# Two-layer hybrid decoder trunk: the MLP's up products as Strassen block products

## The chip, the cores and the metric
The kernel runs on one core of one Trainium2 chip. The metric is the device time of one execution in microseconds (us); lower is better. TensorE is called PE here, VectorE DVE, ScalarE ACT, GpSimd POOL, SyncE SP.

## The reference, cut to what matters
1024 prompt tokens and 32 sample tokens (T = 1056 in all) of 1024 features pass an even layer (GLA and S5 mixer) and an odd layer (conv and RG-LRU mixer). Behind each mixer stands the part that is changed here:

```python
def channel_mixer(x, g_norm, w_up, w_down):
    h = jnp.square(jax.nn.relu(rmsnorm(x, g_norm) @ w_up))
    return h @ w_down        # w_up (1024, 4096), w_down (4096, 1024), float32
```

## The kernel before, in words
Features lie on the 128 partitions: the residual `X` is 8 rows (KT) of 1056 token columns, cut into 3 chunks of CH = 352. A float32 product is made of three passes in a rounded type: with x = XH + XL and w = WH + WL, it adds WH*XH, WH*XL and WL*XH. ACT makes the rounded part (`hi`), DVE the rest (`lo_w`, a subtraction). Inside `product` each matmul has a 128x128 weight block and 352 columns.

Weights come as 128x1024 tiles from one stream in HBM into `WR`, two raw slots. SP waits until a slot's tile has been split (semaphore `w_ready`) and loads the next. The split parts lie in `WH` and `WL`, four slots. Each layer's MLP is 4096 hidden units, 32 tiles of 128 (FT), taken in 16 groups (HG) of two. PE makes the two up tiles (8 weight blocks each, all three chunks), and then the 8 down products of the group before: each adds two hidden tiles into one of 8 output rows. Products go by turns into the two PSUM halves of `acc` (3 banks each). Eight banks exist; `ms` has the other two.

DVE evicts an up product with ReLU and the norm's factor `RS` (`evict`), ACT squares it into `HH`, DVE makes the rest `HL`, and the down products are added to `X` by DVE (`add_to_residual`). Each engine runs its own written order, and semaphores that count up connect them; the groups are hardware loops (`Fori`). The norm's factor per token is computed from squares summed across the rows (`norm_sum`) and is applied after the product, so that the up products can start before it is known.

Ahead of each MLP, `residual(r)` runs on ACT and DVE beside the output projection (`oute`, `outo`, one product for each output row): DVE adds a row, ACT squares it and makes `XH`, DVE makes `XL` and sums the squares. `lam()` makes a small constant of the odd layer and stands before the first MLP.

Of the kernel before, what the change touches and what calls it, by code (L numbers as in the profile page):

```python
# [19 lines left out]
P = 128  # L20
# [67 lines left out]
MLP_TILES = 2 * FT  # L88
ODD_W = ["xb0", "xb1", "xb2"]
for _n in range(1, KT):  # L90
# [5 lines left out]
               + [f"mlp0_{n}" for n in range(MLP_TILES)]  # L96
               + ODD_W
               + [f"outo{m}" for m in range(KT)] + [f"mlp1_{n}" for n in range(MLP_TILES)])
# [8 lines left out]
for _n in range(KT):  # L107
    if _n < KT - 1:
# [5 lines left out]
            + [f"mlp0_{n}" for n in range(HG * (2 + KT))] + _odd + [f"outo{m}" for m in range(KT)]  # L114
            + [f"mlp1_{n}" for n in range(HG * (2 + KT) - KT)])
S5R = index(["ab0t", "ab0r", "cd0a", "cd0b", "ab1t", "ab1r", "cd1a", "cd1b", "ef0a", "ef0b", "ab2t", "ab2r",
             "cd2a", "cd2b", "ef1a", "ef1b", "ab3t", "ab3r", "cd3a", "cd3b", "ef2a", "ef2b", "ef3a", "ef3b"])
M0 = STREAM["mlp0_0"]
# [5 lines left out]
for _name, _n in (("norm0", KT), ("z", 4), ("zg", 4), ("o", 4), ("norm1", KT), ("norm2", KT),  # L124
                   ("mix", 8), ("norm3", KT)):
    SPLIT[_name] = _at
    _at += _n
# [20 lines left out]
def trunk_kernel(nc, x_t, w_stream, par_d, par5_d, cst_d, w_a2, w_ri, st_gla, odd_lru, odd_conv,  # L148
# [8 lines left out]
    with ExitStack() as ctx:  # L157
# [22 lines left out]
        WL = sb(ctx, "WL", [P, SLOTS, 1024], F32R)  # L180
        TT = sb(ctx, "TT", [P, 4, T])
        par = sb(ctx, "par", [P, NPAR])
        cst = sb(ctx, "cst", [P, NCST])
# [56 lines left out]
        XP = sb(ctx, "XP", [P, 3 + SEQ + 7 * NB])  # L240
        WRI = sb(ctx, "WRI", [P, 2, 2, P])
# [3 lines left out]
        CN = sb(ctx, "CN", [P, KT, 3 * (1 + NB)])  # L245
        acc = ctx.enter_context(nc.psum_tensor("acc", [P, 2, NCH, 512], F32))
# [57 lines left out]
        h_sq, h_ready = sem("h_sq"), sem("h_ready")  # L304
# [71 lines left out]

        ident, tri = c_("ident"), c_("tri").rearrange("p (i n) -> p i n", i=NBL)
# [21 lines left out]
        def _(sp):  # L399
# [5 lines left out]
            sp.dma_start(cst[:, :], cst_d).then_inc(cst_in, 16)  # L405
# [118 lines left out]
            at = POOL_LOADS  # L524
            while (NT - at) % 4:
                load_w(at, at % RAW)
                at += 1
            with sp.Fori(0, (NT - at) // 4) as i:
                for j in range(4):
                    n = at + j  # L530
                    split_wait(sp, n - RAW, i * 4)
                    sp.dma_start(WR[:, n % RAW, :], w_stream[i * 4 + n]).then_inc(w_in[n % RAW], 16)
# [9 lines left out]
        @block.gpsimd  # L542
        def _(pool):
            for n in range(POOL_LOADS):
                if n == STREAM["eo1"]:
                    done_wait(pool, "glu3")
                    pool.memset(QM[1][:, :], 0.0).then_inc(qm_zero, 1)
                if n >= RAW:
                    split_wait(pool, n - RAW)
                pool.dma_start(WR[:, n % RAW, :], w_stream[n]).then_inc(w_first[n % RAW], 16)  # L550

            for m in range(1, KT):
# [8 lines left out]
        def _(pe):  # L561
# [394 lines left out]

            def mlp(layer, r):
                w0, t0 = STREAM[f"mlp{layer}_0"], ACC[f"mlp{layer}_0"]
                h0 = FT * layer
                flat = lambda x: 0  # L960
                HOPS = [(lambda k, b=b: HH[:, b + k, :], lambda k, b=b: HL[:, b + k, :]) for b in (0, 2)]

                def up(n, t, per, xn=None, ks=None):

                    split_wait(pe, n, per(4))
                    if t >= 2:
                        pe.wait_ge(acc_read[t % 2], per(5) + t // 2)
                    product(t, lambda k: n % SLOTS, lambda k: k * P, XOPS, xn=xn, ks=ks)

                def down(hready, half, base_w, base_t, per):  # L970

                    split_wait(pe, base_w + 1, per(4))
                    pe.wait_ge(h_ready, hready)
                    for m in range(KT):
                        t = base_t + m
                        pe.wait_ge(acc_read[t % 2], per(5) + t // 2)
                        product(t, lambda k: (base_w + k) % SLOTS, lambda k: m * P, HOPS[half], nk=2)

# [14 lines left out]
                def last_down(hready, base_w, base_t):  # L993

                    split_wait(pe, base_w + 1)
                    pe.wait_ge(h_ready, hready)
                    for c in range(NCH):
                        for m in range(KT):
                            q = c * KT + m
                            b = q % 6  # L1000
                            if q in (0, 3):
                                t = base_t - 2 + (base_t + b // 3) % 2
                                pe.wait_ge(acc_read[t % 2], t // 2 + 1)
                            if q >= 6:
                                pe.wait_ge(fin_read, q - 5)
                            for k in range(2):
                                for i, (w, x) in enumerate(PASSES):
                                    last = mm(acc[:, b // 3, b % 3, 0:CH], w[:, (base_w + k) % SLOTS, m * P:(m + 1) * P],
                                              HOPS[1][x](k)[:, cols_of(c)], k == 0 and i == 0, k == 1 and i == 2)
# [8 lines left out]
                up(w0, t0, flat, SPLIT[f"norm{r}"], ORDER if r == 1 else None)  # L1018
                norm_sum(r)
                up(w0 + 1, t0 + 1, flat)  # L1020
                with pe.Fori(0, HG // 2 - 1) as i:
                    per = lambda x: i * (2 * x)
                    for j in range(2):
                        for e in range(2):
                            up(w0 + 2 + 4 * j + e, t0 + 2 + 10 * j + e, per)
                        down(i * 4 + (h0 + 2 * j + 2), j, w0 + 4 + 4 * j, t0 + 4 + 10 * j, per)
                a = HG - 2
                for e in range(2):
                    up(w0 + 2 + 4 * a + e, t0 + 2 + 10 * a + e, flat)
                down(h0 + 2 * a + 2, 0, w0 + 4 + 4 * a, t0 + 4 + 10 * a, flat)  # L1030
                if layer == 0:
                    down(h0 + 2 * a + 4, 1, w0 + 6 + 4 * a, t0 + 12 + 10 * a, flat)
                else:
                    last_down(h0 + 2 * a + 4, w0 + 6 + 4 * a, t0 + 12 + 10 * a)
# [14 lines left out]

            project("xb0", "xb0", xn=SPLIT["norm2"])  # L1050
            norm_sum(2)
# [19 lines left out]
        def last_down(layer, k):  # L1071

            return f"mlp{layer}_{2 * HG + KT * (HG - 1) + k}"

        X_FROM = [None, None, lambda k: last_down(0, k), lambda k: f"outo{k}"]
# [8 lines left out]
        def _(act):  # L1084
# [39 lines left out]

            def residual(r):

                def square(i, k):
                    if i >= 4:
                        act.wait_ge(ssq_add, SSQ_N * (r - 1) + i - 3)
                    act.activation(TT[:, (i - 1) % 3 if i else 3, :], X[:, k, :], ACT.Square).then_inc(sq_done, 1)  # L1130
# [4 lines left out]
                if r == 1:  # L1135
                    for j in range(KT):
                        if j == KT - 1:
                            for e in range(4, KT - 1):
                                act.wait_ge(x_free, e - 3)
                                x_hi(e, ORDER[e])  # L1140
                        read_wait(act, f"oute{j}")
                        if j < 4 or j == KT - 1:
                            x_hi(j, ORDER[j])
                        square(j, ORDER[j])
                        if j % 2:
                            hi(M0 + j // 2)
                else:
                    for m in range(KT):
                        if r == 3 and m == KT - 1:
                            for k in range(KT - 1):  # L1150
                                act.wait_ge(x_free, 3 + KT - 1 + k + 1)
                                x_hi(k, k)
                        read_wait(act, X_FROM[r](m))
                        if r == 2 and m == 0:
                            act.wait_ge(h_ready, FT)
                        if r == 2 or m == KT - 1:
                            x_hi(m, m)
                        square(m, m)
                        if r == 3:
                            hi(STREAM[f"outo{m}"] + SLOTS)  # L1160
                if r == 2:
                    hi(M0 + MLP_TILES + 2)
                    hi(M0 + MLP_TILES + 3)
# [7 lines left out]
            def last_norm():  # L1171
# [8 lines left out]
                act.wait_ge(h_ready, 2 * FT)  # L1180
# [301 lines left out]
            def mlp(layer):  # L1482
                w0, t0, h0 = STREAM[f"mlp{layer}_0"], ACC[f"mlp{layer}_0"], FT * layer

                def hidden(t, per5, hcount, slot, u, first=False):

                    act.wait_ge(acc_read[t % 2], per5 + (t // 2 + 1))
                    act.activation(HH[:, slot, :], TT[:, u, :], ACT.Square).then_inc(h_sq, 1)  # L1488
                    if not first:
                        act.wait_ge(h_ready, hcount - 1)  # L1490
# [1038 lines left out]
```

## Time and profile before

| | |
|---|---|
| runs | 2280.03, 2280.75, 2290.98 us (median 2280.75) |
| profiled execution, its span | 2288.8 us (the page gives no other time for it) |
| PE busy | 2258.5 us, 13982 matmuls |
| DVE busy | 1198.0 us |
| ACT busy | 648.3 us |
| POOL busy | 23.1 us, 39 instructions |
| HBM traffic | 120.62 MB read, 18.99 MB written |

The span is the time from the first to the last recorded instruction of one execution. Busy times of different engines lie beside each other and are not to be added. A matmul's recorded duration (some 320 ns) is longer than the distance to the next one, since they are pipelined: the rate is read from a chain piece's length divided by its count.

### The profile page before, as it was taken

The page shows a single profiled execution, that of the slowest core. Times are in us where ns is not written, and L with a number is a line of the kernel's source. Part 1 is how long each engine was busy: PE and PEld are TensorE (multiplying, and loading weights), DVE is VectorE, ACT ScalarE, POOL GpSimd, SP SyncE. Part 2 cuts the span into 40 slices and gives each one's busy share as a digit, 9 for nine tenths or more (in the row PEclk, how much of TensorE's full clock was granted, in tenths as well). Part 3 has the DMA queues.
Part 4 walks back from the last instruction along what each step waited for, and adds up shares of the span by engine and source line. Part 5 has one row for each costly group of instructions (what it writes and reads, how often), then busy time and mean ns, then how long its engine had stood idle before and what let it go on. Part 6 is the DMA issues. An engine that isn't in the chain of part 4 may idle for free.

```text
span 2288.8 us, 32453 instructions
## 1 busy us (share of the span) xinstructions
PE 2258.5 (99%) x13982; PEld 2195.0 (96%) x13982; DVE 1198.0 (52%) x1338; ACT 648.3 (28%) x706; POOL 23.1 (1%) x39
## 2 busy tenths in 40 slices
PE   8999999999999999999999999999999999999997
PEld 8998788999999999999999998999999999999996
DVE  8777675644443444344458766544444434443445
ACT  5323632541111111111125556242111111111113
POOL 0000000000000000000000000000000000000001
PEclk9999999999999999999999999999999999999999
DMA  4334224511111111111111111111111111111102
GB/s 173 110 98 135 86 73 132 183 46 46 46 47 45 46 46 40 51 46 46 37 56 40 42 51 40 52 38 50 43 46 46 40 51 46 46 37 55 46 28 76
DMA packets 59129, 140.69 MB, mean 61 GB/s; under 512 B 6416, under 2 KB 30640, under 8 KB 59056
## 3 DMA queue, kind: packets, MB, share of 16 engines
q1 hardware_dynamic: 52720, 121.84, 16.4%
q0 software_dynamic: 3888, 14.16, 1.8%
q10 hardware_dynamic: 2448, 3.64, 0.5%
q8 instruction: 56, 0.92, 0.2%
q14 instruction: 17, 0.14, 0.0%
HBM read 120.62 MB, written 18.99 MB: 61 GB/s over the span
## 4 chain that ended last, share of the span: by engine, by line
PE 93%; DVE 4%; ACT 1%; issue 1%; DMA 0%; DVEq 0%; POOL 0%; ACTq 0%; POOLq 0%
PE acc L563 88%; PE ms L563 2%; DVE TT L1617 1%; PE acc L812 1%; DVE XL L1620 0%; DMA WR<-in_w_stream 0%; PE acc L890 0%; PE ms L660 0%; PE acc L827 0%; PE ms L617 0%; PE acc L823 0%; PE acc L835 0%; DVE XL L1617 0%; DVE HB L2362 0%; DVE X L1620 0%
## 5 line engine op out<-in xcount | busy, mean ns | idle before, releaser
L563 PE MATMUL acc<-XH,WH 128*128 128x352 f32 x2608 | 853.4, 327 | 9.2 <-ACT XP L1239 2.5
L563 PE MATMUL acc<-XL,WH 128*128 128x352 f32 x2608 | 840.0, 322 | 0.0
L563 PE MATMUL acc<-XH,WL 128*128 128x352 f32 x2584 | 833.9, 323 | 0.0
L1617 DVE TENSOR_TENSOR X<-X,acc 128x1056 f32<-128x1056 f32 (+1 forms) x288 | 343.2, 1193 | 370.6 <-PE acc L563 370.6
L563 PEld LDWEIGHTS acc<-XH,WH 128*128 128x128 f32 x2608 | 492.0, 189 | 21.9 <-issue 15.9
L563 PE MATMUL acc<-HH,WH 128*128 128x352 f32 x1536 | 496.6, 323 | 1.4 <-DVE X L1617 1.4
L563 PE MATMUL acc<-HH,WL 128*128 128x352 f32 x1536 | 495.9, 323 | 0.0
L563 PE MATMUL acc<-HL,WH 128*128 128x352 f32 x1536 | 495.3, 322 | 0.0
L563 PEld LDWEIGHTS acc<-XL,WH 128*128 128x128 f32 x2608 | 494.6, 190 | 0.2
L563 PEld LDWEIGHTS acc<-XH,WL 128*128 128x128 f32 x2584 | 487.3, 189 | 0.0
L1114 ACT ACTIVATE WH<-WR 128x1024 fp32r<-128x1024 f32 x177 | 182.8, 1049 | 624.0 <-PE acc L563 561.6
L1620 DVE SCALAR_TENSOR_TENSOR TT<-acc,RS 128x1056 f32<-128x1056 f32 x64 | 80.5, 1257 | 418.8 <-PE acc L563 410.3
L563 PEld LDWEIGHTS acc<-HH,WH 128*128 128x128 f32 x1536 | 288.4, 188 | 3.1 <-issue 1.7
L563 PEld LDWEIGHTS acc<-HL,WH 128*128 128x128 f32 x1536 | 288.3, 188 | 1.3
L563 PEld LDWEIGHTS acc<-HH,WL 128*128 128x128 f32 x1536 | 288.6, 188 | 0.0
L1488 ACT ACTIVATE HH<-TT 128x1056 fp32r<-128x1056 f32 x64 | 69.6, 1087 | 584.5 <-DVE TT L1620 584.5
L1617 DVE TENSOR_TENSOR WL<-WR,WH 128x1024 fp32r<-128x1024 f32 (+1 forms) x179 | 214.8, 1214 | 23.3 <-ACT WH L1114 22.7
L1617 DVE TENSOR_TENSOR HL<-TT,HH 128x1056 fp32r<-128x1056 f32 x64 | 80.3, 1255 | 72.4 <-ACT TT L1491 72.4
L1491 ACT ACTIVATE TT<-TT 128x1056 f32<-128x1056 f32 x64 | 68.4, 1069 | 0.0
L1130 ACT ACTIVATE TT<-X 128x1056 f32<-128x1056 f32 x24 | 25.9, 1078 | 66.5 <-DVE X L1617 66.5
L1620 DVE SCALAR_TENSOR_TENSOR XL<-X,par,XH 128x1056 fp32r<-128x1056 f32 x32 | 41.0, 1312 | 5.8 <-ACT XH L1087 3.2
L1617 DVE TENSOR_TENSOR TT<-TT 128x1056 f32<-128x1056 f32 x29 | 36.4, 1256 | 12.6 <-ACT TT L1130 12.2
(337 smaller groups left out, 1337.1 us busy)
## 6 DMA issues: line engine op xcount, KB each, us to landing
WR<-in_w_stream SPq DMA_DIRECT2D x152, 512.0 KB, 3.3
WR<-in_w_stream POOLq DMA_DIRECT2D x27, 512.0 KB, 4.1
X<-in_x_t SPq DMA_DIRECT2D x8, 528.0 KB, 9.6
LA<-in_x_t SPq DMA_DIRECT2D x24, 176.0 KB, 2.5
xz_scratch<-LA SPq DMA_DIRECT2D x24, 176.0 KB, 1.8
X<-xz_scratch SPq DMA_DIRECT2D x8, 528.0 KB, 5.6
out_y_t<-X SPq DMA_DIRECT2D x12, 352.0 KB, 2.4
u_scratch<-UR SPq DMA_DIRECT2D x4, 576.0 KB, 3.0
```

The lines of the kernel that those rows point to most:

```text
L563: return pe.matmul(out, lhs, rhs, start=start, stop=stop)
L812: last = pe.matmul(glb[0:keys, GLB[b], i * 2 * BL:(i + 1) * 2 * BL], KX[:, b, i * GC:i * GC + keys], QM[p][:, at:at + 2 * BL], start=True, ...
L1114: act.activation(WH[:, n % SLOTS, :], WR[:, n % RAW, :], ACT.Copy).then_inc(w_hi, 1)
L1130: act.activation(TT[:, (i - 1) % 3 if i else 3, :], X[:, k, :], ACT.Square).then_inc(sq_done, 1)
L1488: act.activation(HH[:, slot, :], TT[:, u, :], ACT.Square).then_inc(h_sq, 1)
L1491: act.activation(TT[:, 2 + u, :], TT[:, u, :], ACT.Square).then_inc(h_sq, 1)
L1617: return dve.tensor_tensor(out, a, b, op)
L1620: return dve.scalar_tensor_tensor(out=out, in0=a, scalar=scalar, in1=b, op0=op0, op1=op1)
```

## The change: Strassen's seven products in place of eight for two token chunks
For the up products the 8 weight blocks (K) of a hidden tile pair are cut into halves of 4, the two hidden tiles are the rows, and token chunks 0 and 1 the columns of a 2 by 2 block product. In Winograd's form it takes 7 products of 4 blocks each. Chunk 2 is computed as before (`p1` and `p2`, for tile 0 into bank `B_F0`, for tile 1 into `B_F1`). Four of its eight weight units are sums or differences of blocks; POOL makes them, four per group. Three of the products add up in one PSUM bank `B_CHAIN` in a row, and ACT copies the bank (`snapshot`) between them; the products in `B_P24` and `B_P3` are added to these copies by DVE (`c11`, `c12`, `p5`, `c22`, `c21`), which then applies ReLU.

The token operands (36 parts of 352 columns, some of them differences of chunks and rows) are made once per layer in `residual_mlp`, which takes the place of `residual` before an MLP. Parts lie in the rows of `XH` and `XL` and in spare places.

Weights are now split in units of 512 columns into a ring of 6 half tiles in three of the four slots of `WH`/`WL`. A group has 12 units: 8 up (u0 to u7), 4 down (d0 to d3). The two raw slots have names F0 and F1, and the MLP has a stream of its own (`w_mlp`). The squares of the hidden tiles and their rounding have become two ACT steps, and only one pair of hidden tiles is kept. `lam()` and the loads of the odd layer's states stand after the first MLP.

The diff, cut to its core and set in the order of the engines:

```diff
+        def up_source(j):
+            return (W_A11, W_SUM, W_A12, W_SUM, W_SUM, W_A11, W_A21, W_A22)[j]
+        def down_source(j):
+            return WR[:, :, 2 * P * j:2 * P * (j + 1)]
+F0, F1 = 1, 0
+AFTER = {"u0": 2, "u1": 3, "u2": 5, "u3": 6, "u4": 7, "u5": 8, "u6": 9, "u7": 11,
+         "d0": 13, "d1": 15, "d2": 17, "d3": 19}
+        W_A11, W_A12 = WR[:, F0, 0:UNIT], WR[:, F0, UNIT:2 * UNIT]
+        W_A21, W_A22 = WR[:, F1, 0:UNIT], WR[:, F1, UNIT:2 * UNIT]
@@ SP @@
+                def load(slot, n, units):
+                    sp.wait_ge(u_ready[layer], units)
+                    sp.dma_start(WR[:, slot, :], w_mlp[layer, n]).then_inc(raw_in[layer][slot], 16)
+                with sp.Fori(0, HG - 2) as i:
+                    load(F0, i * 4 + 4, i * STEP_UNITS + (8 + 6))
+                    load(F1, i * 4 + 5, i * STEP_UNITS + (8 + 8))
+                    load(F0, i * 4 + 6, i * STEP_UNITS + (8 + 12))
+                    load(F1, i * 4 + 7, i * STEP_UNITS + (8 + 12))
...
@@ POOL @@
+                def sums(units, earlier, raws, count):
+                    pool.wait_ge(raw_in[layer][F1], raws)
+                    if earlier is not None:
+                        pool.wait_ge(u_ready[layer], earlier)
+                    pool.tensor_tensor(W_SUM, W_A21, W_A22, ALU.add).then_inc(u_sum, 1)
+                    pool.wait_ge(u_ready[layer], units + 2)
+                    pool.tensor_tensor(W_SUM, W_SUM, W_A11, ALU.subtract).then_inc(u_sum, 1)
+                    pool.wait_ge(u_ready[layer], units + 4)
+                    pool.tensor_tensor(W_SUM, W_A12, W_SUM, ALU.subtract).then_inc(u_sum, 1)
+                    pool.wait_ge(u_sum, count)
+                    pool.tensor_tensor(W_A11, W_A11, W_A21, ALU.subtract).then_inc(u_sum, 1)
...
@@ PE, one group: 11 segments of 4 blocks x 3 passes (waits left out) @@
+                    segment(B_CHAIN, u0, "b11", True, False, True, wait=first)
+                    segment(B_F0, u0, "p1", True, False, wait=first)
+                    segment(B_CHAIN, u0 + 1, "t1", False, False, True, wait=first)
+                    segment(B_P24, u0 + 2, "b21", True, True, wait=first)
+                    segment(B_F0, u0 + 2, "p2", False, True, wait=first)
+                    segment(B_CHAIN, u0 + 3, "t2", False, False, True, wait=first)
+                    segment(B_P3, u0 + 4, "b22", True, True, wait=first)
+                    segment(B_CHAIN, u0 + 5, "t3", False, True, True, wait=first)
+                    segment(B_F1, u0 + 6, "p1", True, False)
+                    segment(B_P24, u0 + 7, "n4", True, True, wait=first)
+                    segment(B_F1, u0 + 7, "p2", False, True)
...
+                    down(16, units + 8, lambda m: evs + (3 if m == 0 else 6 if m == 1 else 5 + m), i * 2 + 2)
@@ PE, first group, before its first p1 @@
+                        read_wait(pe, "oute7" if layer == 0 else "outo7")
...
@@ ACT, one group (hi: round a unit; m + n waits for segment n, from 12 on for down products) @@
+                    for u in range(2):
+                        rounded(u, i * 2 + (u + 1), m)
+                    snapshot(layer, 0, m + 1, e)
+                    up_hi(layer, 5, 13, m, None, i * 4 + 4)
+                    up_hi(layer, 6, 14, m + AFTER["u0"], i * 32 + 32, None)
+                    snapshot(layer, 1, m + 3)
+                    up_hi(layer, 7, 15, m + AFTER["u1"], i * 32 + 32, None)
+                    snapshot(layer, 2, m + 6)
+                    down_hi(layer, 0, 16, m + AFTER["u2"], i * 32 + 48)
+                    down_hi(layer, 1, 17, m + AFTER["u3"], i * 32 + 48)
+                    down_hi(layer, 2, 18, m + AFTER["u4"], i * 32 + 48)
+                    squared(0, i * 2 + 3)
+                    down_hi(layer, 3, 19, m + AFTER["u5"], i * 32 + 48)
+                    following(0, "u6")
+                    following(1, "u7")
+                    squared(1, i * 2 + 4)
+                    following(2, "d0")
...
@@ DVE, one group (up_lo, unit_lo: the rest of a unit) @@
+                    c11(m, e, n)
+                    f0(m)
+                    unit_lo(layer, 16, u + 9, down_source(0))
+                    unit_lo(layer, 17, u + 10, down_source(1))
+                    c12(m, e, n)
+                    unit_lo(layer, 18, u + 11, down_source(2))
+                    p5(n)
+                    c22(m)
+                    unit_lo(layer, 19, u + 12, down_source(3))
+                    following(0)
+                    c21(m, e)
+                    following(1)
+                    f1(m, e)
+                    add(0)
+                    add(1)
+                    following(2)
...
@@ DVE, residual_mlp: after their add rows 0 to 3 get front(j), rows 4 to 7 temps(j - 4) @@
+                    add_to_residual(order[j], ACC[name])
...
+                    if j == KT - 2:
+                        for i in range(4):
+                            rest(i)
+                        for i in range(3):
+                            pair(i)
+                pair(3)
...
-            residual(1, ACC["oute0"])
+            residual_mlp(1)
+            mlp(0)
+            residual(2)
+            link(dve.memset(XP[:, 0:3], 0.0))
             lam()
```

`front` makes 3 parts or temps, `temps` 4, `rest` 1, `pair` 5. In `following(j)` the unit is u(j) of the next group, in the last group d(j).

## Rows read from the trace of the kernel before

**Rows 1.** The page, section 1: busy us (share of the span) xinstructions.
```profile
PE 2258.5 (99%) x13982; PEld 2195.0 (96%) x13982; DVE 1198.0 (52%) x1338; ACT 648.3 (28%) x706; POOL 23.1 (1%) x39
```

**Rows 2.** The chain of waits: start us, us, what.
```profile
482.93 2.04 PE ms L617 x6
484.97 725.82 PE acc L563 x4536
...
1538.54 702.69 PE acc L563 x4392
```

**Rows 3.** One group by stretch: us, busy (x) by engine, PEclk, DMA share, GB/s.
```profile
560.00:606.08 46.08, 46.08 (x290) 46.08 (x290) 19.53 (x16) 8.04 (x8) 0.00 (x0) 1.00 0.14 46
```

**Rows 4.** Groups by line and shape: busy us, mean ns | idle before us, releasers.
```profile
L1617 DVE TENSOR_TENSOR X<-X,acc 128x1056 f32<-128x1056 f32 x264 | 331.0, 1254 | 362.8 <-PE acc L563 362.8
...
L1620 DVE SCALAR_TENSOR_TENSOR X<-X,par,RS 128x352 f32<-128x352 f32 x24 | 12.7, 578 | 11.9 <-ACT RS L1178 11.9
...
L1617 DVE TENSOR_TENSOR X<-X,acc 128x352 f32<-128x352 f32 x24 | 12.2, 518 | 7.8 <-PE acc L563 7.8
L1190 ACT ACTIVATE TT<-X 128x352 f32<-128x352 f32 x24 | 11.8, 498 | 36.6 <-DVE X L1617 32.5 <-PE ms L563 3.6 <-POOL TT L557 0.5
...
L1617 DVE TENSOR_TENSOR XP<-acc,RS 128x704 f32<-128x704 f32 x8 | 7.1, 884 | 0.0
...
L557 POOL TENSOR_TENSOR TT<-TT 128x352 f32<-128x352 f32 x7 | 6.6, 947 | 1870.6 <-ACT TT L1190 1869.7
...
L1277 ACT ACTIVATE WH<-WR 128x512 fp32r<-128x512 f32 x1 | 0.6, 632 | 0.7 <-DMA WR<-in_w_stream 0.7
...
L1617 DVE TENSOR_TENSOR WL<-WR,WH 128x512 fp32r<-128x512 f32 x2 | 1.3, 685 | 0.0
```

**Rows 5.** Timeline, DVE and SyncE at 604 us: start us, us, engine, operation, [idle before].
```profile
603.55 1.26 DVE L1617 TENSOR_TENSOR HL<-TT,HH 128x1056 fp32r<-128x1056 f32 x1 [2.13 <-ACT TT L1491]
604.73 1.22 DVE L1617 TENSOR_TENSOR WL<-WR,WH 128x1024 fp32r<-128x1024 f32 x1
...
606.12 0.33 SPq L532 DMA_DIRECT2D WR<-in_w_stream  x1
```

**Rows 6.** Raw loads by tile, at 605 to 625 us and at 636 to 650 us.
```profile
DMA to landing us min/median/max: 3.1/3.2/3.2
...
L532 SPq DMA_DIRECT2D WR<-in_w_stream x2: 333/333/333, 637.2 to 638.3; - x2
...
DMA to landing us min/median/max: 3.2/3.8/4.5
```

**Rows 7.** Stretches with PE idle and after (columns as Rows 3), and the chain.
```profile
47.30:50.20 2.90, 0.02 (x1) 0.00 (x0) 2.80 (x4) 2.33 (x2) 0.53 (x1) 1.00 0.31 82
51.00:61.20 10.20, 10.20 (x38) 9.18 (x37) 9.72 (x17) 4.29 (x8) 0.53 (x1) 0.50 0.15 51
1416.60:1419.10 2.50, 0.04 (x2) 0.03 (x1) 1.38 (x2) 2.49 (x3) 0.00 (x0) 1.00 0.00 0
1419.70:1423.10 3.40, 3.40 (x13) 3.40 (x12) 0.40 (x1) 2.85 (x4) 0.00 (x0) 0.50 0.33 124
2241.20:2242.70 1.50, 0.06 (x2) 0.08 (x1) 1.25 (x1) 0.00 (x0) 0.00 (x0) 1.00 0.00 0
2242.70:2260.00 17.30, 17.30 (x101) 16.45 (x102) 6.78 (x13) 9.27 (x16) 6.63 (x7) 1.00 0.01 1
...
1419.10 13.33 PE acc L563 x72
```

**Rows 8.** Timeline of DVE before each MLP (columns as Rows 5).
```profile
465.88 1.25 DVE L1617 TENSOR_TENSOR X<-X,acc 128x1056 f32<-128x1056 f32 x1 [0.92 <-PE acc L563]
...
473.15 1.24 DVE L1617 TENSOR_TENSOR X<-X,acc 128x1056 f32<-128x1056 f32 x1
...
1513.65 1.25 DVE L1617 TENSOR_TENSOR X<-X,acc 128x1056 f32<-128x1056 f32 x1 [6.64 <-PE acc L563]
```

**Rows 9.** Waits of DVE: line waited for, us in total, times, longest.
```profile
DVE sp L2309 <- ACT spt L1517: 10.1, 1, 10.1
```

More of the change, by code:

```diff
@@ L963, in up, with segment @@
[L963 to L973, printed above, removed]
-                    for m in range(KT):
-                        t = base_t + m
-                        pe.wait_ge(acc_read[t % 2], per(5) + t // 2)
-                        product(t, lambda k: (base_w + k) % SLOTS, lambda k: m * P, HOPS[half], nk=2)
+                def segment(out, unit, name, start, stop, chain=False, wait=False):
+                    for i in range(4):
+                        if wait:
+                            pe.wait_ge(xs_ready, X_PARTS * layer + X_COUNT[name](i))
+                        hi, lo = (xs(layer, name, i, part) for part in range(2))
+                        for j, (w, x) in enumerate(((WH, hi), (WH, lo), (WL, hi))):
+                            last = pe.matmul(out, ring(w, unit)[:, i * P:(i + 1) * P], x, start=start and i == 0 and j == 0,
+                                             stop=stop and i == 3 and j == 2, skip_group_check=chain)
+                    last.then_inc(mark[layer], 1)
@@ L1482, in mlp @@
             def mlp(layer):
[L1483 to L1490, printed above, removed]
-                    act.activation(TT[:, 2 + u, :], TT[:, u, :], ACT.Square).then_inc(h_sq, 1)
@@ L1512, in lam @@
+                for u in range(2):
+                    rounded(u, FT - 1 + u, LAST_MARK)
+                if layer == 0:
+                    hi(POOL_LOADS)
             def lam():
@@ L1527, in _ @@
             load_ri(1)
-            mlp(0)
             residual(2)
+            lam()
             def decays_of(n):
@@ new lines, in mlp @@
+                up_lo(layer, 6, 6, 7)
+                up_lo(layer, 7, 7, 8)
+                dve.wait_ge(ssq_add, SSQ_N * r)
+                c11(0, 0, 0)
+                dve.wait_ge(rs_ready, 1 + 2 * layer)
+                f0(0)
+                for i in range(4):
+                    x_rests(r)[4](i)
+                up_lo(layer, 0, 8, 9)
+                up_lo(layer, 1, 9, 10)
+                c12(0, 0, 0)
+                up_lo(layer, 2, 10, 11)
+                p5(0)
+                c22(0)
@@ new lines, in mlp, with last_norm @@
+                up_lo(layer, 3, 11, 12)
+                up_lo(layer, 4, 12, 13)
+                c21(0, 0)
+                f1(0, 0)
+                with dve.Fori(0, HG - 2) as i:
+                    step.loop(i, 1)
+                    turn(i)
+                step.end(HG - 2)
+                turn(HG - 2, True)
+                for x in range(2):
+                    hidden_lo(x, FT - 1 + x)
+                if layer == 0:
+                    lo_w(POOL_LOADS)
+            def last_norm():
```

664 lines of the change are left out of this document (464 added, 200 removed).

## The prediction, made before the changed kernel had run
> **What bounds the kernel now.** I read the page first: TensorE (PE) is busy 99% of a span of 2288.8 us [rows 1]. A busy PE says little about its rate, so the chain of waits comes next: in both MLP stages it is one unbroken piece of matmuls, 4536 in 725.82 us and 4392 in 702.69 us [rows 2], both 0.160 us each. The reader is to see that nothing else stands inside these pieces. By stretches, one group of hidden units (2 up tiles, 8 down products, 288 matmuls) lasts 46.08 us with PE busy throughout, DVE 19.5, ACT 8.0 and POOL nothing [rows 3]. So a matmul saved in the MLP is worth its full 0.160 us as long as no other engine comes late, and a wait that PE does not have today is paid in full.
>
> **Matmuls removed.** An up group has 2 tiles x 8 blocks x 3 passes x 3 chunks = 144 matmuls. Strassen leaves 11 segments x 4 blocks x 3 passes = 132. Over 16 groups and 2 layers that is 384 fewer, at 0.160 us: **-61.4 us**. All have 352 columns as before. A group becomes 132 + 144 = 276 matmuls, 44.16 us; a segment is 1.92 us, one down product (18 matmuls) 2.88 us.
>
> **Load of the other engines.** Durations from [rows 4]: DVE makes the rest of 512 columns in 0.69, adds a product of 1056 columns in 1.25, one of 352 in 0.52, works on 704 in 0.88. Per group DVE has 12 half tiles (8.2), 8 adds (10.0), 2 hidden rests (2.5), nine 352-column steps (4.7) and one of 704 (0.9): 26 us of 44. ACT has 12 x 0.63, 3 x 0.50 and four over 1056 columns at some 1.0 each (8.04 for the eight whole-tile operations in [rows 3]): 13 us. POOL has 4 sums of 512 columns. No engine is full, so capacity does not decide; the order within one group does.
>
> **The new wait in each group.** Down product 1 writes the PSUM bank that holds the second tile's chunk 2 (`B_F1`), so it waits for DVE's `f1`. DVE does `f1` behind `following(1)`, the rest of unit u1 of the *next* group. That unit is rounded from the sum W21+W22, which POOL makes only when the next raw tile is in slot F1, and SyncE loads it only when DVE has finished d3, the last down unit, since d3 reads both raw slots. Take t = 0 at the end of segment 8 (`t3`); PE then has segments 9 to 11 and down product 0 to do: 3 x 1.92 + 2.88 = 8.64 us. The chain beside it, with an operation that follows another without a wait starting 0.08 before its end (603.55 + 1.26 against 604.73 [rows 5]):
> - ACT's third snapshot waits for segment 6 (t = -3.84, hand-over 0.2 taken for the matmul's tail): 0.50, then d0 rounded, 0.54: t = -2.60.
> - DVE, all queued behind each other: d0 0.05 + 0.69, d1 0.61, c12 0.44, its relu 0.04 + 0.88, d2 0.61, p5 0.44, c22 twice 0.44, d3 0.61: t = 2.65.
> - SyncE issues 0.17 after DVE's end (605.95 to 606.12 [rows 5]), F0 first at 2.82, F1 0.4 later.
> - The pair lands. One load alone takes 3.2 from issue; of two issued 1.1 apart the second takes 4.5 from its own issue, 5.6 from the first [rows 6]. At 0.4 apart I take 5.0 from the first: t = 7.8. Ends: 3.7 (0.4 + one load alone, no sharing at all) and 5.8.
> - POOL: 7 adds of 352 columns took 947 ns each [rows 4]. For 512 columns: between 0.95 (no dependence on length) and 1.38 (in proportion), and up to 2.0 if DVE is in its way; I take 1.38, since the row's inputs and output are in the same memory: t = 9.3.
> - ACT 0.05 + 0.63, DVE 0.05 + 0.69, f1 0.44, hand-over 0.15: t = 11.3.
> So PE stands 11.3 - 8.64 = **2.7 us** before down product 1, in every one of the 14 groups per layer with a successor; the ends give 0.9 to 4.1. The wait renews itself each time, because the chain starts from that group's own segment 6. In the last group unit 21 is a down unit without a POOL sum: 2.7 - 1.4 = 1.3, twice 1.3 = **+2.6**.
>
> The Trainium skill ("GPSIMD Engine Reference", section "3.1 Elementwise — side-by-side cycle accounting") gives 4497 ns for a float32 add of 2048 columns; 160 columns more than the row's 352 would by that slope, as an estimate, cost 0.35, so 1.30 a sum, and the total would be 2 us lower. The Trainium skill ("DMA: Bandwidth & Descriptors", "Anatomy of one DMA — SWDGE (gpsimd) path") fits a transfer as 2.0 us plus its bytes at 436 GB/s; two tiles as one stream would land 4.4 us after issue, 0.6 sooner than I take, and the total would be 17 us lower. The pair in [rows 6] was slower than that, 5.6, so the trace doesn't agree.
>
> **The clock after a wait.** After its start PE four times stood idle for 1.8 to 2.9 us, and each time the granted clock then fell to 0.50 (1.2 of 2.4 GHz); two of the four stand in [rows 7]: after 2.46 us idle 3.4 us at half, as after the other two, and after 2.9 even 10.2 us. A wait of 1.5 us was followed by a full clock [rows 7]. After the 2.46 the chain has 72 matmuls in 13.33 us [rows 7] where 0.160 each makes 11.52: 1.8 more, of which 0.1 is the pipe filling. So each wait of 2.7 us costs a further **1.7 us**. Ends: 0 if it passes as the 1.5 did, 5.1 (half of 10.2) if it goes as after 2.9. Per group 4.4, and 28 groups: **+123.2 us**.
>
> **Start of each MLP.** PE's first `p1` needs the bank of the last output product, so DVE's add of row 7. DVE now does `rest` x4 and `pair` x3 ahead of it: 19 parts of 352 columns at 0.50 (0.58 less 0.08, as above [rows 4]). Layer 0: add 6 began at 465.9 [rows 8]; add 1.2, four temps of 352 columns 2.1 (from 0.52 to 0.58 each in [rows 4]), square sum 1.2, parts 2.0 + 7.5, then add 7, 1.2: 481.1. PE ends oute7 where the norm sum starts, 482.93, less the 72 matmuls of the first up tile [rows 2]: 471.4; b11 ends at 473.3: it waits 8.0. Before, add 7 stood at 473.15 [rows 8], and the first up tile began at once, on the other bank. Layer 1: add 6 at 1513.65 [rows 8]; units 4 and 5 add 1.3; the rows are freed one by one within outo7, soon enough; add 7 ends at 1530.2. PE ends outo7 at 1538.54 - 2.04 - 11.52 = 1525.0 [rows 2], b11 at 1526.9: 3.3. With 1.7 of clock each: **+14.7**, ends 0 (parts at ACT's and DVE's slack) and 22. The square sum for the norm is then ready as `t1` ends.
> In the first group the weight sums 1 to 3 of the second follow one another through POOL, ACT and DVE (unit u4 at 18 us after `t1`), ahead of c21 and f1: PE waits 1.1 before the second `b11` and 0.8 for its snapshot, which stands behind two roundings: **+3.8** for both layers, ends 0 and 8.
>
> **After layer 0.** `lam()` now stands between the norm and the first `take_xb`. Before, DVE lost 10.05 to it in the MLP [rows 9], where PE did not notice. There it costs DVE the part of this that is ACT's Exp and a table load, and five small steps, taken together as 2.5, with some slack in the next product: **+2.0**, ends 0 and 3.
>
> **At nothing.** The number of raw tiles and bytes is the same. The ring of six half tiles is refilled at least six segments (11 us) ahead but for u1 above, against 1.4 us for ACT and DVE. Snapshot 0 ends 1.1 before `t1` wants it; h is ready 10 us before its down products; down product 2 wants add 0, which follows f1 by 1.7 of 2.88. The final norm keeps its steps. If the snapshot's 1.1 goes, it costs its excess 30 times.
>
> **Sum:** -61.4 + 123.2 + 2.6 + 14.7 + 3.8 + 2.0 = +84.9. The profiled span of 2288.8 is 8 above the median of 2280.75; the difference is carried to the median: **2366 us**, slower by 3.7%.
>
> **Rivals.**
> - *The clock holds.* 2.7 us of idleness lies above the longest that passed (1.5), below the 2.9 that cost most. It would be 84.9 - 47.6 - 3.4 = +34: 2315. Four of four speak against it. 0.14.
> - *The raw tile comes in time* (faster). If d3, the pair, the sum, ACT and DVE take 2.7 less, the wait is gone: -61.4 + 14.7 + 3.8 + 2 = -41: 2240. Landing in 3.7 and a sum in 0.95 give 1.7 of the 2.7; the rest would have to come from DVE's queue of nine steps. From a chain below 8.64 it decides. 0.08.
> - *Near no change.* A wait of 0.9 to 1.2 at a full clock: -61.4 + 28 x 1.0 + 20 = -13, 2268, or up to 2290. 0.06.
> - *POOL is slower or blocked* (2.0 and more beside DVE), or the pair takes 5.8: wait 4.1: +39: 2405. 0.08.
> - *The long half clock*, as after 2.9: 28 x 3.4 more: 2461. 0.06.
> - The forecast: 0.58.
>
> The range leaves out the two ends, some 2 in 10: 2310 to 2405. About 0.5%, 11 us, is what a measurement of this kernel can tell from no change. Faster: 0.08 and a part of the third, 0.10; same 0.04; slower 0.86.
>
> **What would show it.** In the profile after: 13598 matmuls; in the MLP a group of 48 to 49 us; per group one PE wait of 2.7 us before the down product on `X<-X,acc`, put down to DVE; then 3.4 us at 0.50; POOL adds of 1.3 to 1.4 us, the first some 0.1 after a raw tile's landing; an 8 us gap before the first `p1` of layer 0. A group of 44.2 us, or a granted clock of 1.00 in the MLP, would make the forecast wrong.

## The result, and the profile after

The changed kernel took 2372.85 us (median of 4 runs, 2366.81 to 2380.95), the kernel before beside it 2285.86 (4 runs, 2280.03 to 2291.33). The ratio is 1.0378, 95% interval 1.0344 to 1.0412: slower by 3.8%, where 2366 us and 3.7% were forecast. The profiled execution took 2380.95 us, its span 2379.2.

The page, busy time by engine and the chain that ended last; it answers to [rows 1]:

```profile
PE 2249.2 (95%) x13598; PEld 2174.5 (91%) x13598; DVE 1437.1 (60%) x1946; ACT 808.0 (34%) x1115; POOL 187.8 (8%) x167
...
PE 68%; DVE 12%; DMA 7%; issue 6%; ACT 4%; POOL 2%; SPq 1%; DVEq 0%; ACTq 0%; POOLq 0%
```

The 384 matmuls are gone, but the span grew by 90 us: PE was busy 99% of its span and is now busy 95%. A third of the chain is no longer PE's. What PE waits for (engine, line, waited for: us in total, times, longest):

```profile
PE acc L681 <- DVE TT L1906: 72.8, 30, 3.9
PE acc L1089 <- DVE X L1903: 10.1, 1, 10.1
PE acc L681 <- issue: 3.7, 1, 3.7
PE acc L681 <- DVE HL L1903: 3.7, 1, 3.7
```

L681 holds the down products' matmuls, and L1906 is the DVE helper behind `f1`: one wait in each of 30 groups, 72.8 us in all. Three groups in a row, from one such wait's end to the next one's (columns as [rows 3]), answer to [rows 3]:

```profile
541.62:590.88 49.26, 46.89 (x276) 46.59 (x276) 25.83 (x33) 12.53 (x19) 5.13 (x5) 0.95 0.14 43
590.88:639.50 48.62, 46.17 (x277) 45.88 (x277) 25.84 (x33) 12.53 (x19) 5.16 (x5) 0.96 0.14 43
639.50:686.40 46.90, 44.62 (x277) 44.33 (x277) 25.88 (x33) 12.54 (x19) 5.19 (x5) 1.00 0.14 45
```

A group lasted 46.08 us before. In the 26 groups that end with a wait of this size it is now 46.7 to 47.1 us where the clock stays at 1.00, and 48.1 to 49.3 where it falls, though a group needs 12 matmuls fewer. DVE is busy for 26 us of it and ACT for 12.5, as forecast, so neither is full. The chain of waits through the second of these waits (start us, us, what):

```profile
574.14 1.94 PE ms L1089 x12
576.10 0.04 ACT TT L1364
...
576.47 0.62 ACT WH L1297
...
581.80 0.69 DVE WL L1903
...
582.66 0.33 SPq L599
...
583.18 4.39 DMA WR<-in_w_mlp
...
587.75 1.27 POOL cst L650
589.04 0.64 ACT WH L1297
...
590.31 0.53 DVE TT L1906
590.84 0.04 issue
590.88 1.37 PE acc L681 x4
```

To be read from the top: segment 6 ends at 576.10, the third snapshot and d0 follow on ACT, DVE works down its queue to d3 (581.80), SyncE issues, the pair lands at 587.57, POOL adds, ACT rounds, DVE makes the rest and then does `f1`. PE had nothing from 588.51 to 590.88. This is the forecast's chain link by link.

### The profile page after: what moved, and what is told of

Same layout as the page of the kernel before. It is cut to its first block, busy times and chain, and to the rows that moved or that the text cites. A ratio compares the mean times of both kernels' runs of the same rounds, so it can differ in the third digit from the quotient of the medians.

```text
span 2379.2 us, 34746 instructions
## 1 busy us (share of the span) xinstructions
PE 2249.2 (95%) x13598; PEld 2174.5 (91%) x13598; DVE 1437.1 (60%) x1946; ACT 808.0 (34%) x1115; POOL 187.8 (8%) x167
## 4 chain that ended last, share of the span: by engine, by line
PE 68%; DVE 12%; DMA 7%; issue 6%; ACT 4%; POOL 2%; SPq 1%; DVEq 0%; ACTq 0%; POOLq 0%
PE acc L681 48%; PE ms L1089 9%; DMA WR<-in_w_mlp 6%; PE acc L1089 5%; DVE TT L1903 3%; DVE WL L1903 3%; PE ms L681 2%; ACT WH L1297 2%; POOL cst L650 2%; DVE TT L1906 1%; DVE XL L1906 1%; PE acc L930 1%; SPq L599 1%; DVE X L1903 1%; DVE HB L1906 1%
## 5 line engine op out<-in xcount | busy, mean ns | idle before, releaser
L681 PE MATMUL acc<-HH,WH 128*128 128x352 f32 x1536 | 516.8, 336 | 80.2 <-DVE TT L1906 72.8
L681 PE MATMUL acc<-HL,WH 128*128 128x352 f32 x1536 | 510.7, 332 | 0.0
L681 PE MATMUL acc<-HH,WL 128*128 128x352 f32 x1536 | 509.1, 331 | 0.0
L1903 DVE TENSOR_TENSOR WL<-WR,WH 128x512 fp32r<-128x512 f32 (+1 forms) x339 | 256.2, 764 | 299.3 <-ACT WH L1297 274.9
L681 PEld LDWEIGHTS acc<-HH,WH 128*128 128x128 f32 x1536 | 300.6, 196 | 90.9 <-DVE TT L1906 81.5
L681 PE MATMUL acc<-XH,WH 128*128 128x352 f32 x1072 | 358.3, 334 | 11.9 <-ACT XP L1498 2.5
L681 PE MATMUL acc<-XL,WH 128*128 128x352 f32 x1072 | 348.0, 325 | 0.0
L681 PE MATMUL acc<-XH,WL 128*128 128x352 f32 x1048 | 340.9, 325 | 0.0
L681 PEld LDWEIGHTS acc<-HL,WH 128*128 128x128 f32 x1536 | 300.7, 196 | 1.3
L681 PEld LDWEIGHTS acc<-HH,WL 128*128 128x128 f32 x1536 | 300.3, 195 | 0.0
L1297 ACT ACTIVATE WH<-WR 128x512 fp32r<-128x512 f32 x288 | 176.6, 626 | 259.2 <-DMA WR<-in_w_mlp 155.1
L681 PEld LDWEIGHTS acc<-XH,WH 128*128 128x128 f32 x1072 | 204.5, 191 | 24.9 <-issue 15.6
L1089 PE MATMUL acc<-XH,WH 128*128 128x352 f32 x640 | 207.4, 324 | 13.0 <-DVE X L1903 10.1
L1089 PE MATMUL acc<-XH,WL 128*128 128x352 f32 x640 | 206.9, 323 | 0.0
L1089 PE MATMUL acc<-XL,WH 128*128 128x352 f32 x640 | 206.4, 322 | 0.0
L681 PEld LDWEIGHTS acc<-XL,WH 128*128 128x128 f32 x1072 | 205.5, 192 | 0.2
L681 PEld LDWEIGHTS acc<-XH,WL 128*128 128x128 f32 x1048 | 200.1, 191 | 0.0
L1297 ACT ACTIVATE WH<-cst 128x512 fp32r<-128x512 f32 x96 | 60.6, 632 | 355.0 <-PE acc L681 290.2
L1089 PEld LDWEIGHTS acc<-XH,WH 128*128 128x128 f32 x640 | 120.6, 188 | 13.6 <-issue 13.6
L1089 PE MATMUL ms<-XH,WH 128*128 128x352 f32 x384 | 124.1, 323 | 0.0
```

The costliest lines, as they stand in the source:

```text
L681: return pe.matmul(out, lhs, rhs, start=start, stop=stop)
L1089: last = pe.matmul(out, ring(w, unit)[:, i * P:(i + 1) * P], x, start=start and i == 0 and j == 0, stop=stop and i == 3 and j == 2, skip_g ...
L1297: act.activation(out, source, ACT.Copy).then_inc(u_hi[layer], 1)
L1903: return dve.tensor_tensor(out, a, b, op)
```

## The experiments

All ratios are to the kernel before, with 95% intervals. "After" is the changed kernel.

**e1: `f1` ahead of the next group's unit u1.** The disputed order by itself.

```diff
                     following(0)
                     c21(m, e)
-                    following(1)
                     f1(m, e)
                     add(0)
+                    following(1)
                     add(1)
```

> DVE takes f1 and add 0 ahead of following(1), nothing else moves. Theory (PE waits for f1, and f1 stands behind the rest of u1, which stands behind d3, the raw pair and the POOL sum): f1 is done 0.7 us after segment 11, so the 28 waits of some 2.4 us and the half clock behind 18 of them go; u1 of the next group is ready at 10.7 us after t3, needed at 31.7. A group goes from 46.9 to 48.6 down to 44.2 us, the time by 28 x 2.4 + 18 x 1.7 = 98 us to some 2275, ratio to the kernel before 0.995. Rival A (DVE as a whole is late, the order does not matter): the wait moves to down product 2, which needs add 0, or to the next group's b11, and the time stays within 20 us of 2373. Rival B (the raw tile is late for everything): a wait of some 2 us at the next group's t1.

Measured: 2275.09 us, ratio 0.9952 [0.9929, 0.9975]. That is 98 us below after's median, by one line on DVE's queue, and with it the change becomes a gain, if one of 0.5% only. One group of e1 (columns as [rows 3]):

```profile
523.00:567.20 44.20, 43.99 (x274) 43.99 (x274) 24.66 (x32) 12.43 (x19) 4.56 (x5) 1.00 0.16 48
```

That is the 276 x 0.160 = 44.16 us of the matmul count: in this group no wait is left and the clock is full. Ahead of the down products four waits of 1.0 to 1.7 us stay, in the first and the last group of each layer. The raw pair, POOL's sum and u1 are as late as before the edit; only `f1` no longer stands behind them.

**e2: the wait filled.** 14 matmuls without use, into the free bank `B_CHAIN`, between down products 0 and 1.

```diff
+                        if m == 1 and fill:
+                            pe.wait_ge(evict[layer], evs(0) + 1)
+                            for _ in range(FILL):
+                                pe.matmul(B_CHAIN, ring(WH, u0)[:, 0:P], HH[:, 0, 0:XW], start=True, stop=True)
                         pe.wait_ge(evict[layer], evs(m))
```

> PE runs 14 matmuls of 352 columns into the chain bank, whose content is used up by then, between down products 0 and 1; they add to nothing that is read. They take 14 x 0.16 = 2.2 us of the 2.4 us that PE waits. Theory of the clock (idleness over some 1.8 us is what makes the granted clock fall, and the fall costs 1.7 us each time): the wait stays in place of 2.4 us as matmuls, PEclk is 1.00 in all groups, every group lasts 46.6 to 46.9 us, and the time falls by 18 x 1.7 = 31 us to some 2342, ratio 1.025. Rival (the half clock costs nothing, since the group's length is set by the chain of DVE, SyncE, POOL and ACT and PE catches up): within 5 us of 2373, ratio 1.038. Rival (it is no matter of idleness): PEclk still falls in the groups.

Measured: 2337.88 us, ratio 1.0236 [1.0194, 1.0278]. 14 x 0.160 = 2.24 us of work lies where the 2.4 us wait was, and a stretch of 45 us across a group has a full clock:

```profile
540.00:585.00 45.00, 44.85 (x280) 44.56 (x279) 24.99 (x31) 12.55 (x19) 5.14 (x4) 1.00 0.15 47
```

None of the 28 groups of e2 shows a half clock, and they follow each other at 46.9 us (median), as after's groups do at a full clock: the useless matmuls take the time of the wait and no less. With PE's lost time left in place and its idleness taken away, 35 us go (2372.85 to 2337.88). The half clocks in after's groups are worth 31 of it by the account below; the other 4 are within the interval (0.4% either way, 10 us).

**e3: the tile that POOL waits for loaded first.** Of the pair, SyncE issues F1 ahead of F0.

```diff
-                    load(F0, i * 4 + 6, i * STEP_UNITS + (8 + 12))
                     load(F1, i * 4 + 7, i * STEP_UNITS + (8 + 12))
+                    load(F0, i * 4 + 6, i * STEP_UNITS + (8 + 12))
```

> SyncE issues the load of slot F1 (which the POOL sum needs) ahead of slot F0, for the pair of up tiles alone. Theory: the sum starts 1.0 to 1.3 us sooner, but u0, which stands ahead of u1 on ACT and DVE, now waits for the second landing; from that landing the chain has ACT 0.63 + 0.55, DVE 0.7, f1 0.5, in place of POOL 1.27 + ACT 0.63 + DVE 0.7 + f1 0.5. The wait falls by some 0.8 us to 1.6, below the shortest after which the clock fell, so the clock falls in few groups: 28 x 0.8 + 15 x 1.7 = 48 us less, 2325, ratio 1.017. If the clock falls as often as before: 2350. Rival A (DVE as a whole is late): no change, 2373.

Measured: 2352.94 us, ratio 1.0303 [1.0261, 1.0345]. The row of the waits:

```profile
PE acc L681 <- DVE TT L1906: 59.4, 30, 3.2
```

In a group the wait fell from 2.4 to some 1.9 us. The tile of F1 did come sooner: POOL's sum starts 3.8 us after the end of d3, where it was 5.3 (medians 3.84 and 5.25). But the chain of waits now goes past POOL, over the tile of F0, which is issued second (columns as above):

```profile
573.91 4.39 DMA WR<-in_w_mlp
...
578.32 0.64 ACT WH L1297
...
578.99 0.05 DVE WL L1903
...
579.60 0.08 DVE TT L1903
...
580.03 0.68 DVE WL L1903
580.71 0.45 DVE TT L1906
```

That is the landing, ACT's rounding and DVE's rest of u0, then `c21`, the rest of u1 and `f1`: 2.9 us from the landing to PE. The expectation had named this turn, but without u0's rest and `c21` on DVE, and so took 2.4. The gain of 1.4 us at POOL comes to PE as 0.5. The half clock followed 13 of the 28 waits, so the expected low end (2325) missed and the other value named (2350) came.

**e4: POOL's first sum made twice.** It adds one POOL operation to the chain and changes no value.

```diff
+                    pool.tensor_tensor(W_SUM, W_A21, W_A22, ALU.add).then_inc(u_twice, 1)
+                    pool.wait_ge(u_twice, turn)
                     pool.tensor_tensor(W_SUM, W_A21, W_A22, ALU.add).then_inc(u_sum, 1)
```

> POOL makes the first of the four sums twice. Theory (the sum is a link of the chain, one to one): each of the 28 waits grows by one sum and one hand-over, 1.3 to 1.4 us, to 3.8, and the clock falls after all 28 in place of 18, perhaps for 6.8 us where the wait crosses over: 28 x 1.35 = 38 us at the least, with 10 x 1.7 more 55 us: 2410 to 2430, ratio 1.055 to 1.065. Rival (POOL's sums are hidden, the wait is the DMA's or DVE's alone): no change.

Measured: 2432.74 us, ratio 1.0671 [1.0614, 1.0728], 60 us above after.

```profile
PE acc L683 <- DVE TT L1908: 108.2, 30, 5.0
```

The 28 waits with a sum in their chain grew from 69.3 to 104.7 us, 1.26 each: one POOL sum (1.28 here) arrived at PE in full. The two in the last groups, which have none, stayed at 1.9 and 1.6. The other 25 us of the 60 are the clock: a half clock followed all 28, and after 10 of them it lasted 6.8 us instead of 3.4. PE worked 117 us of these groups at half, 61 in after, and half of the difference is 28 us.

**e5: e1, and the last hidden pair rounded early.** After's profile had a wait that the forecast lacked: 3.7 us ahead of each layer's last down products, because the last pair's roundings overwrite `HH` and so wait for the last mark, and because DVE makes their rests behind the last add. The chain there (columns as above), with the rests of two hidden tiles between the last add and PE:

```profile
1228.93 5.33 PE acc L681 x33
1234.25 0.02 issue
1234.28 1.25 DVE X L1903
1235.53 2.35 DVE HL L1903 x2
1237.88 0.04 issue
1237.92 2.13 PE acc L681 x6
```

e5 gives this pair two free slots of `HH` and `HL`, and its rests a place ahead of the last two adds; it changes both at once and doesn't tell them apart.

```diff
                 for u in range(2):
-                    rounded(u, FT - 1 + u, LAST_MARK)
+                    rounded(u, FT - 1 + u, LAST_MARK - DOWN_MARKS, 2)
...
                     following(4)
+                    if last:
+                        hidden_lo(0, FT - 1, 2)
                     add(6)
+                    if last:
+                        hidden_lo(1, FT, 2)
                     add(7)
```

> On top of e1_f1_ahead: the last pair of hidden tiles goes into tiles 2 and 3 of HH and HL, whose token parts are used up once the last up segments are done, so it is rounded during the down products before and not after them. Theory: the wait of 3.7 us ahead of the last down products (once per layer, the step that the prediction left out) is two roundings and two rests behind mark LAST_MARK; both waits and the half clock behind them go, 2 x 3.7 + 2 x 1.7 = 10.8 us less than e1_f1_ahead: 2264, ratio 0.990. Rival (the wait is for the bank or the last weight units): it stays and the time is that of e1_f1_ahead.

Measured: 2261.77 us, ratio 0.9912 [0.9881, 0.9943]; once more beside e9: 2267.12 us, ratio 0.9920 [0.9895, 0.9944]. Both waits are gone from the trace. The time is 0.3 to 0.4% below e1's ratio of 0.9952, 7 to 9 us, with intervals that touch. What this last run was expected to show:

> The kernel of e5 once more, on the chip and in the rounds of e9, since what stands between the two is under 0.2%. Expected 0.991 of the time before (2260 to 2264 us), inside e5's first interval of 0.9881 to 0.9943; above 0.9943 would say that the earlier difference between e5 and e8 was partly that of chips.

**e6: e1, and the parts of rows 4 to 7 made behind add 7, in the order of the segments.** It was to take away the wait at the MLP's start. DVE's side of it, which ACT follows:

```diff
                         for i in range(4):
                             rest(i)
-                        for i in range(3):
-                            pair(i)
-                pair(3)
+                for name in ("b21", "p2", "t2", "b22", "t3"):
+                    pair(name)
```

> On top of e1_f1_ahead: ahead of each MLP the 20 parts of rows 4 to 7 are made after the add of row 7, in the order in which PE's segments use them (all b21, all p2, ...), and the third snapshot stands ahead of the norm's Ln. Theory: p1 of layer 0 waits for the bank that add 7 frees, and add 7 stands behind 15 parts: the wait of 9.2 us there and the half clock of 10.2 us behind it (5.1) go, in layer 1 the wait of 2.9; perhaps 2 us each come back at the norm or the first group. Between 10 and 17 us less than e1_f1_ahead: 2258 to 2265, ratio 0.988 to 0.991. Rival (the parts themselves are what PE waits for, so that their order only moves the wait to b21): no more than 3 us less.

Measured: 2283.48 us, ratio 0.9999 [0.9981, 1.0017]. A miss, and worse than e1 by 0.5%. The wait ahead of the first `p1` fell from 9.2 to 3.3 us, and others came in its place:

```profile
PE ms L1089 <- DVE TT L1905: 9.2, 2, 5.2
PE ms L1089 <- DVE WL L1905: 5.0, 2, 2.9
...
PE acc L1089 <- DVE X L1905: 3.3, 1, 3.3
```

PE now reaches `n4` and the second group's `b11` earlier than the norm's factor, POOL's sums and `c21` are there: the early wait had covered the later ones. The waits of both starts add up to 17.5 us, where e1 has 18.1. But a half clock followed each of the five, and 24 us of PE's work fell into it, against 4 us in e1: 10 us more, about what the time lost. This fits a start that is bound by all that ACT and DVE have to do there and not by its order; no run made that work less, so it isn't shown.

**e7: e1, and lam()'s second part behind the first `take_xb` and `conv`.**

```diff
+            def lam_rest():
                 dve.wait_ge(lam_act, 1)
...
                 lo_w(STREAM[f"xb{n}"] + SLOTS)
+                if n == 0:
+                    lam_rest()
```

> On top of e1_f1_ahead: the second part of lam() on DVE, which waits for ACT's Exp and table load, stands behind the first take_xb and conv. Theory: take_xb 0 starts 2.2 us sooner, PE's waits of 1.45 and 0.68 us at the start of the odd layer shrink or go, 1 to 2.5 us less than e1_f1_ahead; too little for the time alone, the waits in the profile decide. Rival (the late start of xb0, 1.5 us, sets it): the waits stay.

Measured: 2275.11 us, ratio 0.9952 [0.9934, 0.9970]. In the trace a wait of 1.45 us at the odd layer's start is gone, in the time no difference from e1 can be told.

**e8: e5, e6 and e7 together, and `c21`, `f1` ahead of the rests of u3 and u4 in the first group.**

```diff
                 c22(0)
-                up_lo(layer, 3, 11, 12)
-                up_lo(layer, 4, 12, 13)
                 c21(0, 0)
                 f1(0, 0)
+                up_lo(layer, 3, 11, 12)
+                up_lo(layer, 4, 12, 13)
```

> e5, e6 and e7 together on top of e1_f1_ahead, and in each layer's first group c21 and f1 ahead of the rests of u3 and u4. If the causes are separate and add up: 10.8 + 14 + 2 + 3 = 30 us less than e1_f1_ahead's 2275, some 2245 to 2250, ratio 0.983 to 0.985. The matmuls saved are worth 61.4 us (ratio 0.973); what stays is the gaps in the first groups, the norm and the late bank of xb0. Rival (what is won in one place comes back in the next): 2260 or more.

Measured: 2267.94 us, ratio 0.9929 [0.9905, 0.9952]: short of the expected 2245 to 2250, and no better than e5. Waits at the start of layer 0: 2.4, 2.1, 1.6 and 2.9 us, of layer 1: 2.1 and 3.1, so e6's trade again.

**e9: e8 without e6's order.**

```diff
+                        for i in range(3):
+                            pair(i)
-                for name in ("b21", "p2", "t2", "b22", "t3"):
-                    pair(name)
+                pair(3)
```

> e5 with two more edits of order on DVE: in the first group c21 and f1 stand ahead of the rests of units u3 and u4, and the second part of lam stands behind the first take_xb and conv. The parts of residual_mlp stay in their old order. In e5 the first group waits 1.32 us ahead of the second b11 in layer 0 (495.8 to 497.1) and 1.98 in layer 1 (1536.4 to 1538.4). My theory: both go to DVE's queue, and both disappear (DVE is two steps of 0.69 us further ahead, and unit u4 was not what the snapshot waited for), so 2260 less 2.8 to 3.3 us, some 2257 to 2259, ratio 0.989 to 0.990, and below e5 in the same comparison. Rival: the second b11 waits for the chain u3, u4, POOL's sums, c21 in another order, so that it needs u4 of the ring anyway and the wait stays in place or moves behind b11 as it did in e8 (2.86 us there): the time is that of e5 or 1 to 4 us above it.

Measured: 2266.60 us, ratio 0.9904 [0.9878, 0.9931]; e5's kernel beside it 0.9920 [0.9895, 0.9944]. The two can't be told apart, and the rival was right: the waits of the first group (1.3 and 1.8 us, 2.0 and 1.3) merged into one of 3.3 us in each layer, now for ACT's snapshot, which stands on ACT's queue behind u4's rounding, a square and a hidden rounding; 3.4 us at a half clock followed each. Its chain in layer 0:

```profile
506.08 1.29 POOL cst L654
...
507.46 0.08 ACT WH L1297
...
508.00 1.07 ACT TT L1745
...
509.95 1.07 ACT HH L1750
511.01 0.36 ACT TT L1364
511.37 0.04 issue
511.41 3.83 PE ms L1089 x13
```

The best version measured is e5 or e9, some 0.9% below the kernel before.

## Why the prediction was right

**Matmuls: -61.4, right.** 13598 are counted. Where nothing waits (e1), a group is 44.20 us by 44.16 forecast.

**The wait in each group: mechanism right, size 2.4 for 2.7.** From t = 0 at 579.94 (576.10 plus two segments of 1.92): the rest of d3 ends at t = 2.55 (2.65 forecast), the pair has landed at 7.63 (7.8), POOL ends at 9.08 (9.3), PE goes on at 10.94 (11.3), and it was idle from 8.57 (8.64). From the first issue to the landing it is 4.9 us, where 5.0 was taken. The chain came out 0.4 shorter by small parts: 0.10 up to the end of d3, 0.07 for issue and landing, 0.05 for POOL with its hand-over, 0.14 from there to PE. POOL's sum by itself:

```profile
L650 POOL TENSOR_TENSOR cst<-WR 128x512 f32<-128x512 f32 x32 | 41.1, 1285 | 1338.4 <-DVE WL L1903 837.7 <-DMA WR<-in_w_mlp 500.7
```

1.29 us against 1.38 by proportion from [rows 4]: it has a fixed part. The Trainium skill ("GPSIMD Engine Reference", section "3.1 Elementwise — side-by-side cycle accounting") gives 4497 ns for 2048 columns; the estimate by that slope was 1.30, and the trace agrees with it. The 28 groups with a successor lost 69.3 us (75.6 forecast), the first of each layer 3.9 and 3.7 of it; the last groups lost 1.8 and 1.7 (1.3 forecast each). e1 shows that `f1`'s place is the cause; e4 shows that POOL's sum is a link of its chain, by making it longer, and e3 that the raw pair is one: with the order of the two tiles turned the wait hangs on the other tile and is 0.5 shorter.

**The clock: right in kind, not each time.** The forecast had a half clock after every wait. In the trace it followed 18 of the 28. Two waits of nearly one length, and PE after each (columns as [rows 3]): the wait of 2.37 us that ended at 590.88, and the one of 2.45 that ended at 639.50.

```profile
591.10:594.50 3.40, 3.40 (x13) 3.40 (x13) 2.19 (x2) 1.08 (x1) 0.65 (x1) 0.50 0.00 0
639.50:642.90 3.40, 3.40 (x21) 3.40 (x22) 2.61 (x3) 1.29 (x2) 0.86 (x1) 1.00 0.00 0
```

13 matmuls at 1.2 GHz in the one, 21 at 2.4 GHz in the other. The granted clock was at half for some 61 us of PE's work in the 28 groups, which cost half of it, 30.7 us, against 47.6 forecast. Of the rival *the clock holds* a third came true. Beyond idle time and half clock a group with a wait takes 0.2 to 0.5 us more than its matmuls (46.90 - 2.28 - 44.16 = 0.46 in the third group shown, 0.27 in the mean), where 0.1 was taken: some +8 over the 30 groups.

**Start of each MLP: +14.8 by +14.7 forecast, but by other parts.** Layer 0 waited 10.1 us (9.2 in e1), not 8.0 (7.8 by the forecast's own terms, 481.1 - 473.3). The parts took as long as forecast (add 6 began at 473.4, add 7 ended at 488.4: 14.9 against 15.2), but add 6 itself was 2.6 late against PE: the rows with `temps` take ACT and DVE 5.5 to 5.8 us each and had lost their slack before row 6. This is the step that failed: rows 4 to 6 were priced as if each began on time. The half clock after it was the long one, but it began within the wait, and PE met only its end:

```profile
481.90:488.40 6.50, 0.00 (x0) 0.00 (x0) 6.48 (x13) 2.46 (x6) 0.00 (x0) 0.50 0.00 0
488.48:492.10 3.62, 3.62 (x12) 3.62 (x13) 3.51 (x6) 3.60 (x7) 0.00 (x0) 0.50 0.00 0
```

So it cost 1.8 us. Layer 1 waited 2.9 (3.3 forecast) at a full clock. The first groups' waits, 1.3 and 2.0 with 0.3 each behind them, are the +3.8 forecast; what each waits for was only half right, as e9 shows.

**Left out: 7.4 us of waits and 4.3 of half clock ahead of the last down products.** The text said that h is ready 10 us ahead of its down products. That holds for all groups but the last, whose roundings wait for the mark of the group before. In e5's trace neither wait is left; its time fell by 7 to 9 us against e1, 11.7 by this account.

**lam(): half right in the trace, not seen in the time.** Waits of 1.5, 1.5 and 0.7 us stand at the odd layer's start, some 3 us more than before (2.0 forecast). But the first of them ends with an add to `X` (1263.91 to 1265.16), and lam() begins 12 us later. e7 took the second away, which is lam()'s, and the median didn't move.

**The account:** -61.4 + 69.3 + 30.7 + 5.2 (last groups, one half clock) + 14.8 + 3.9 + 11.7 + 3.0 + 3.4 (6.8 us more at half clock outside the MLPs) + 8 = +88.6; the spans differ by 90.4. The forecast's +84.9 is near it because the clock and the wait of the groups were taken 23 us too high, and the last pair and what a wait costs beyond its idle time left out at 20. That these cancel is luck: its total is better than its terms.

**The rivals.** POOL wasn't slow. The raw tile in time would have needed the chain below 8.64, near no change below some 9.8 (8.64 + 1.2); it was 10.94. What was not among the rivals is e1's answer: the chain may stay as long as it is if nothing that PE needs stands behind it.

## What to carry to other kernels

Before an edit that saves work on the bounding engine, walk each in-order queue for a step that the bounding engine needs and that stands behind one waiting for a long chain; here one step's place was worth 98 us, the saved work 61. A wait moved at a place where two engines are nearly full comes back at the next step (e6, e9), so add up their work up to each point where PE needs them. Look at the first and the last pass of a loop separately: the steady pass had neither the 10.1 us start nor the 3.7 us end.

## What the runs showed of the hardware

**The clock after short waits.** No half clock followed the six waits of 1.0 to 2.0 us in e1's groups. One followed 10 of 22 waits of 1.7 to 2.0 us (e3), 16 of 26 of 2.2 to 2.5 us (after), and all 28 of 3.4 us and more (e4). The length alone doesn't decide: behind e3's two waits of 3.2 us, in its first groups, the clock stayed full. What does was not tried. The forecast had taken four of four from the trace of before, which were waits outside the MLP of 1.8 to 2.9 us. Every run has these same four waits. Behind them the clock fell four times in after too, but only 17 times of 40 in the traces of the ten experiments. In e1, for one, after the wait of 2.46 us that ended at 1409.69 (columns as [rows 3]):

```profile
1409.69:1415.00 5.31, 5.31 (x33) 5.31 (x34) 1.26 (x1) 5.28 (x5) 0.00 (x0) 1.00 0.25 93
```

Whether the clock falls behind a wait of this length is thus a matter of the single execution, and one trace can't price it.

**DVE stands still beside POOL.** Two operations of one form, 352 columns with both tensors in SBUF. In after, the second relu step of `f1` began at 590.86, 0.4 us into POOL's second sum (start us, us, engine, operation):

```profile
590.31 0.52 DVE L1906 SCALAR_TENSOR_TENSOR TT<-acc,RS 128x352 f32<-128x352 f32 x1
590.47 1.27 POOL L652 TENSOR_TENSOR cst<-cst,WR 128x512 f32<-128x512 f32 x1 [1.47 <-DVE WL L1903]
590.86 1.27 DVE L1906 SCALAR_TENSOR_TENSOR TT<-TT,RS 128x352 f32<-128x352 f32 x1
```

It ended at 592.13, 0.39 after POOL's end at 591.74. In e1 the same pair met at another offset:

```profile
567.14 1.27 POOL L650 TENSOR_TENSOR cst<-WR 128x512 f32<-128x512 f32 x1 [30.31 <-DVE WL L1903]
...
567.46 0.52 DVE L1906 SCALAR_TENSOR_TENSOR TT<-acc,RS 128x352 f32<-128x352 f32 x1
568.01 0.79 DVE L1906 SCALAR_TENSOR_TENSOR TT<-TT,RS 128x352 f32<-128x352 f32 x1
```

Here it took 0.79 and ended at 568.80, again 0.39 after POOL's end (568.41), while the operation with one input in PSUM ran beside POOL at its usual 0.52. All 56 such meetings in the two traces end 0.38 to 0.39 us after POOL, with lengths from 0.79 to 1.60 us; the 8 of this operation that met no POOL operation took 0.53. So it waits for POOL to finish and then runs; it isn't slowed in proportion. The Trainium skill ("SBUF — State Buffer", section "Who interferes with whom") states this: a DVE operation with two SBUF inputs and a GpSimd operation that reads SBUF exclude each other for a whole instruction. The trace agrees. It cost nothing here, since PE waits for the first of the two steps only.
